# Output products of a kernel's last stage in halves of 256 columns, with their stationary operands moved apart in SBUF

## The reference

```python
def in_proj(x, g, w):
    p = rmsnorm(x, g) @ w
    ...
def hgrn2_out(o, g, dtype):
    o = rmsnorm(o, g.reshape(H_B, DV_B))
    return o.reshape(*o.shape[:-2], MIX_WIDTH).astype(dtype)
def out_proj(x, mix_o, xq, mk, mv, gate, w):
    y = jnp.concatenate([mix_o, cross_attn(xq, mk, mv)], axis=-1) * jax.nn.silu(gate)
    return x + y @ w
```

## Time and profile before

| | us |
|---|---|
| median of 3 runs | 2384.9 (2383.94 to 2387.3) |
| span of the profiled execution | 2376.1 |
| TensorE busy in the span | 2312.2 (97%) |
| VectorE busy | 1819.5 (77%) |
| ScalarE busy | 1413.5 (59%) |
| last stage, first output product to the last one's start | 1945.5 to 2367.8 |
| products in the last stage | 816 |

### The profile page before, as it was taken

One profiled execution on the slowest core, in us unless ns is written; L12 is line 12 of the kernel. 1 busy time (PEld: TensorE's weight loads), 2 busy tenths in 40 slices (PEclk: granted clock), 3 DMA queues, 4 the chain that ended last, 5 costly groups with the idle time before them and its releaser, 6 DMA issues. The chain is left out here.

```text
span 2376.1 us, 61711 instructions
## 1 busy us (share of the span) xinstructions
PE 2312.2 (97%) x23787; PEld 2094.7 (88%) x23787; DVE 1819.5 (77%) x3555; ACT 1413.5 (59%) x3281; POOL 381.0 (16%) x585
## 2 busy tenths in 40 slices
PE   7999999999989999999999999999999989999998
PEld 4999999999967888888887999999999978888886
DVE  7889788887666656666666998797888777888885
ACT  4564666755565555555554564776757566666664
POOL 2332000000022221211112332000000112112111
PEclk9999999999999999999999999999999999999999
DMA  6886887769894222222226897886879793444442
GB/s 227 298 299 219 301 281 231 247 220 332 232 307 121 83 66 89 90 69 83 73 81 232 272 303 242 256 275 214 266 248 312 230 269 117 129 131 122 137 135 70
DMA packets 396664, 469.64 MB, mean 198 GB/s; under 512 B 39860, under 2 KB 248556, under 8 KB 396376
## 3 DMA queue, kind: packets, MB, share of 16 engines
q1 hardware_dynamic: 379832, 406.02, 54.4%
q0 software_dynamic: 14704, 54.92, 6.6%
q10 hardware_dynamic: 1840, 4.75, 0.7%
HBM read 318.77 MB, written 151.56 MB: 198 GB/s over the span
## 5 line engine op out<-in xcount | busy, mean ns | idle before, releaser
L1468 PE MATMUL pj_acc<-x_lo,pj_wh 128*128 128x256 f32 (+1 forms) x3080 | 780.9, 284 | 0.0
L1468 PE MATMUL pj_acc<-x_hi,pj_wh 128*128 128x256 f32 (+1 forms) x3080 | 780.8, 284 | 0.0
L1468 PEld LDWEIGHTS pj_acc<-x_hi,pj_wh 128*128 128x128 f32 x3080 | 578.4, 188 | 0.0
L1468 PEld LDWEIGHTS pj_acc<-x_lo,pj_wh 128*128 128x128 f32 x3080 | 578.4, 188 | 0.0
L509 ACT ACTIVATE pj_wh<-pj_wt 128x512 fp32r<-128x512 f32 x676 | 420.3, 634 | 255.9 <-DMA pj_wt<-tsum 175.1
L516 DVE SCALAR_TENSOR_TENSOR pj_wl<-pj_wt,pj_wh 128x512 fp32r<-128x512 f32 x676 | 467.0, 708 | 87.0 <-ACT pj_wh L509 79.3
L1464 PE MATMUL pj_acc<-x_hi,pj_wl 128*128 128x256 f32 (+1 forms) x3080 | 509.4, 287 | 13.8 <-DVE pj_wl L516 11.9
L1464 PEld LDWEIGHTS pj_acc<-x_hi,pj_wl 128*128 128x128 f32 x3080 | 425.3, 188 | 22.1 <-DVE pj_wl L516 19.5
L1307 DVE TENSOR_TENSOR pj_out<-pj_out,pj_acc 128x512 f32<-128x512 f32 (+1 forms) x448 | 320.8, 716 | 103.3 <-PE pj_acc L1468 69.7
L2541 DVE COPY pb_pt<-pb_SCTP 128x256 f32<-128x256 f32 (+2 forms) x266 | 115.8, 435 | 147.5 <-PE pb_SCTP L2352 74.3
L2676 ACT ACTIVATE pb_se<-pb_se,pb_mn 128x640 f32<-128x640 f32 (+4 forms) x208 | 154.6, 745 | 114.6 <-DVE pb_mn L2524 114.3
(11 more groups left out here) (371 smaller groups left out, 3992.1 us busy)
## 6 DMA issues: line engine op xcount, KB each, us to landing
pj_wt<-tsum SPq DMA_DIRECT2D x546, 256.0 KB, 3.8
proj<-pj_out SPq DMA_DIRECT2D x112, 512.0 KB, 4.2
tsum<-pj_wt SPq DMA_DIRECT2D x140, 256.0 KB, 3.2
pj_wraw<-in_w_in_dram POOLq DMA_DIRECT2D x24, 1024.0 KB, 6.6
tsum<-pj_wraw SPq DMA_DIRECT2D x56, 256.0 KB, 4.2
hg_x<-x_mid SPq DMA_DIRECT2D x17, 512.0 KB, 3.7
pb_gate<-proj SPq DMA_DIRECT2D x16, 512.0 KB, 5.1
pb_x<-in_x_prompt_dram SPq DMA_DIRECT2D x16, 512.0 KB, 3.8
```

Source lines behind the costliest of these rows:

```text
L1468: ins = nc.tensor.matmul(BANK[j][:, 0:n], w.hi[j][:, k], x.of(y, p, j)[:, k], start=False, stop=(k == 3 and i == 1))
```

## The change

Each product of 512 columns becomes two of 256, with the same stationary operand: first columns 0 to 255 for the first half, then 256 to 511, each with its own place in the PSUM bank. The bank's start flag stands on the first of the 48 alone and its stop flag on the last. The parts of yh and yl get 16 columns of padding each, so that they lie 576 bytes apart instead of 512; 56 columns of padding stand ahead of yh and 8 ahead of yl. ScalarE's cast and VectorE's subtraction write four pieces of 128 columns instead of one of 512. Waits, semaphores and the order of the pieces stay.

```diff
-        yh = sb("hg_yh", [P, KD, P], F32R)
-        yl = sb("hg_yl", [P, KD, P], F32R)
+        sb("hg_pad0", [P, 56])
+        yh = sb("hg_yh", [P, KD, P + 16], F32R)[:, :, 0:P]
+        sb("hg_pad1", [P, 8])
+        yl = sb("hg_yl", [P, KD, P + 16], F32R)[:, :, 0:P]
...
-                        cs = slice(half * 512, half * 512 + 512)
                         g = GROUPS[s]
-                        nc.tensor.matmul(to[:], yh[:, s], woh[:, g, cs], start=(s == 0), stop=False)
-                        nc.tensor.matmul(to[:], yh[:, s], wol[:, g, cs], start=False, stop=False)
-                        if s % 4 == 0:
-                            pe.wait_ge(s_yl, 2 * job + s // 4 + 1)
-                        ins = nc.tensor.matmul(to[:], yl[:, s], woh[:, g, cs], start=False, stop=(s == KD - 1))
+                        for part, (a, b) in enumerate(((yh, woh), (yh, wol), (yl, woh))):
+                            if part == 2 and s % 4 == 0:
+                                pe.wait_ge(s_yl, 2 * job + s // 4 + 1)
+                            for at in (0, 256):
+                                ins = nc.tensor.matmul(to[:, at:at + 256], a[:, s], b[:, g, half * 512 + at:half * 512 + at + 256],
+                                                       start=(s == 0 and part == 0 and at == 0),
+                                                       stop=(s == KD - 1 and part == 2 and at == 256))
...
-                    nc.vector.tensor_tensor(yl[:, 4 * c:4 * c + 4].rearrange("p k n -> p (k n)"), y[c][:],
-                                            yh[:, 4 * c:4 * c + 4].bitcast(F32).rearrange("p k n -> p (k n)"),
-                                            ALU.subtract).then_inc(s_yl, 1)
+                    nc.vector.tensor_tensor(yl[:, 4 * c:4 * c + 4], y[c][:].rearrange("p (k n) -> p k n", n=P),
+                                            yh[:, 4 * c:4 * c + 4].bitcast(F32), ALU.subtract).then_inc(s_yl, 1)
...
-                    nc.scalar.copy(yh[:, 4 * c:4 * c + 4].rearrange("p k n -> p (k n)"), y[c][:]).then_inc(s_yh, 1)
+                    nc.scalar.copy(yh[:, 4 * c:4 * c + 4], y[c][:].rearrange("p (k n) -> p k n", n=P)).then_inc(s_yh, 1)
```

## The result

The changed kernel takes **2393.7 us** (median of 5, 2388.3 to 2395.9) where the kernel before, on the same chip, takes 2383.9 us (2381.9 to 2387.3): 1.0042 times as long, 95% interval 1.0030 to 1.0054. The forecast was 2382.5 us, within 0.2% of before, with a range up to 2390.0. The time lies outside it, on the slower side. One run in this document, of the padding alone, took 3215.3 us; it counts as slow and stands in no ratio.

What follows compares the result with a forecast made beforehand. TensorE's own instructions were taken to bound the last stage; -2.9 us for halves with piece entries and +0.5 for supply gave -2.4, from 2384.9 to 2382.5 us, range 2374.0 to 2390.0.

Steps and rivals of the forecast that it cites:

- What bounds the stage: Last stage, about 1945 to 2367.8 us: TensorE's own instructions bind it; product gains or losses reach the span nearly one to one.
- Instruction supply: TensorE's queue: 1632 more instructions, a tenth more, raise "issue" idle in proportion, +0.5 us, bounds -2 to +3.
- The three entries: Largest "issue" waits of TensorE in the last stage, with nothing shown as waited for: 4.4 us before, about 4.9 expected.
- the short pitch: 113.3 ns per 256-column half, from the input projection; expected in the last stage, saving 6.4 ns a product, chance 0.45.
- What a half costs: Last stage's products: halves at 113.3 ns against break-even 116.5, as in the input projection; with piece entries -2.9 us.
- The padding: Moved weight offsets of yh and yl in the last stage: no effect on the products' time, taken as 0.
- The start of a run: Pieces of products after transposes: four halves take 0.56 us against 0.54 for two whole products, 0.01 us dearer a piece.
- Copy and subtraction: ScalarE's and VectorE's writes into padded tiles: under 0.3 us each, covered by TensorE's products, taken as 0.
- (a): Last stage's halves hold 117.8 ns, costing 2.6 ns a product: +3.9 us, 2388.8 us; chance 0.20.
- (b): Last stage: loads and stream no longer meet, halves at 111.8 to 107.5 ns: -5.9 to -12.9 us, middle 2375.5; chance 0.24.
- (c): Last stage: weights' offset jumps between parts, so halves stay at 120 ns: +6.2 us, 2391.1 us; chance 0.11.
- (d): Last stage: two halves share one weight load, so the change does not do what it says; held excluded, no chance given.

Runs made afterwards that it cites:

- the second trace: The changed kernel run and traced once more with no edit, against the kernel before: 1.0041, 2392.1 us.

## Why the prediction was wrong, point by point

- **What bounds the stage** was right. TensorE is at 97%, nothing waits for yh or yl, and what its instructions lost came through: 11.2 us in the stage of the trace, 9.8 in the time.
- **Instruction supply** is the step that failed most. It was taken in proportion, +0.5 us with a bound of +3; it came to +7.6 at line ends, +9.4 in the second trace. The three entries that the prediction named went from 4.4 to 9.1 us, the one at the products from 0.5 to 2.2, and turn_outputs (1.1) joined them. The wrong idea was that a tenth more instructions bring a tenth more idle. A line costs only if it is used up before the next has come. In before a piece of six products holds the queue for 1.4 us with 12 instructions; in halves the same 1.4 us need 24, so that near a burst of levels less time goes by for each line. That is nine of the 16 line ends; why packets start late at others stays open. Halves with the short pitch were 8 us slower than before; with the burst cut they were level with it. "Few and long" had been read, and what they had in common, the ends of lines, had not been asked.
- **What a half costs** was right as a fact of the input projection and wrong as a forecast for the stage; this is the second step that failed. 113.3 ns was taken, 118.3 came: the term of -2.9 us became +2.6 to +3.4 from start to start. Break-even at 116.5 ns held. The entry of a piece was misread a little, too: by the rows shown, 0.56 us against 0.54 is 0.02 us and not 0.01 (0.015 by the unrounded starts), and with 0.02 the term is -2.3.
- **The padding** at 0 was the reason for that. The padding itself added no cost, since halves without it stand at 118.4 ns; what was left out is the difference. The prediction saw that no row showed another difference at 256 columns and that "nothing excludes an effect", and then took 0 from rows of 512 columns. The difference sets the pitch of halves from 113.3 to 120.0 ns. The change's parts go through all eight places, yh's four with two thirds of the halves and yl's four with one, which by the measured list is a mean of 117.9 ns, and 118.3 came. What it said of the input projection, that the offset alone does not decide between its two pitches, was right.
- **The start of a run**: the first four halves after transposes take 0.56 us in the stage too (2024.50 to 2025.06); with the pitch at 118 ns there was nothing to gain from it.
- **Copy and subtraction** at 0: right, the padded layout alone is at 0.9995.
- **The rivals.** (a), the long pitch, came nearest in mechanism: 117.8 against 118.3 ns, 2388.8 us against 2393.7, short because it carried the same 0.5 us of supply. (b) is excluded: no difference gave less than 113.3 ns. (c) came nearest in time, 2391.1 us, for the wrong reason; its moving offset costs nothing by itself. (d) did not occur.
- **The chances.** The range ended at 2390.0 because supply was bounded at +3 us and the dear pitch had too little chance. It took both to miss it: the forecast's own pitch with 7.6 us of supply gives 2389.6, just inside, and the long pitch of (a) with it 2395.9, outside.

## What to carry to other kernels

Before splitting instructions on a queue, look at what its unexplained idle has in common: if it falls at fixed counts of instructions, each split makes lines run out faster, and the price is paid where a line is gone before the next has come, which the mean count does not tell. A pitch read in one stage belongs to that stage's distance between weights and moving operand, modulo 256 bytes, and to how its runs begin; carry it over only with both. And where weights and stream are both in SBUF, trying their distance costs one line: here the time fell by 0.15% with it, while the split raised it by 0.4%.

## What the runs showed of the hardware

- The pitch of a float32r matmul with a fresh load depends on the distance from moving operand to weights modulo 256 bytes: 113.3 to 120.0 ns at 256 columns, 226.7 to 234.4 ns at 512 in long runs. The distance counts and not the weights' place, with four exceptions in the 16 runs that tell them apart.
- At some distances (64, 96, 192 bytes) there is more than one steady pitch; the beginning of a run picks it, and it lasts: 117.8 ns after four transposes, 113.3 after three, five or eight.
- In the last stage TensorE's idle without a releaser falls at the ends of lines of 256 instructions and ends 2.2 to 3.3 us after the start of a 16 KB packet on the instruction queue; 1.0 us or so in the last tile is the exception.
- Behind idle of 2.1 to 2.5 us at a line end (four traces) the granted clock went to 0.50 for 3.4 us, within 1.5 us of its end.
- The Trainium skill, "TensorE: Matmul & The Clock Gate", section "Back-to-back issue gap", gives N/2.4 + 2.5 ns as the gap of a single matmul, by which I estimate 109.2 ns for 256 columns and 215.8 for 512; no difference that was tried came that low (113.3 and 226.7).
